# A 1-core transformer kernel: modulation weights summed by VectorE beside the projections, scores of two heads issued together, prefix products ahead of the decays

## The chip, the cores and the metric

The kernel runs on one core of one Trainium2 chip, in one launch. The metric is the device time in microseconds. Three runs of the kernel before have a median of 2638.65 us (2635.41 to 2647.42). The names used below: PE is TensorE, DVE is VectorE, ACT is ScalarE, POOL is GpSimd, SP is SyncE, which here issues all weight loads.

## The reference, cut to what matters

Two blocks are computed on 256 latent tokens and 256 context tokens of width 1024, all in float32. In both, a small vector `c` of 1024 numbers is multiplied with a large matrix `w_mod` (24 MB per layer), and the result shifts, scales and gates the normalised tokens:

```
mod = silu_c @ w_mod[l] + b_mod[l]
sh1, sc1, gt1, sh2, sc2, gt2 = jnp.split(mod[:, None, :], 6, axis=-1)
h = modulate(rms_norm(x, g_pre1[l]), sh1, sc1)
hc = modulate(rms_norm(ctx, g_pre1[l]), sh1c, sc1c)
qn, kn, vn, qh, zf, zb, ih, gh = split_cols(h @ w_in[l])
...
s_win = jnp.einsum('bhrjqd,bhrjakd->bhrjqak', q_blk, k_blk) * scale
p = jax.nn.softmax(s_all, axis=-1)
...
b = jnp.cumsum(log_f.reshape(bsz, nh, n, HG_CHUNK, dk), axis=3)
q_dec = qc * jnp.exp(b)
k_dec = kc * jnp.exp(-b)
def step(s, inp):
    dec, upd = inp
    return dec[..., None] * s + upd, s
```

The first block is: a projection, an attention of 8 heads of 64 over 512 keys, a recurrence in chunks of 32 tokens and both directions ("hgrn"), a projection back, and 16 experts. The second is a hybrid block (the same kind of attention, a delta rule, a gated feed-forward) and a convolution block with another feed-forward.

## The kernel before

Everything is written out by hand: each engine has its own list of instructions, and they meet through semaphores. Each PE result goes to one of eight banks; `next_bank` takes banks in turn from the first `rotating[0]`, and a bank can be filled again once the engine that reads it has counted up `bank_drained`.

All weights pass through `ring`, which has six slots. SP loads them in one fixed order, a slot of 1 MB (some 1.4 or 1.5 MB) at a time; the load with number n first waits until the slot's last user, number n - 6, is done (`freed_by`), and every later load stands behind it in SP's queue. A projection block (`project`, loop over `IN1_BLOCKS`: eight blocks, of which five use four token tiles and three use two) takes two slots; its first slot is freed in the middle of the block, its second at the block's end.

A modulation weight slot ("tile", rows `k`, third `p` of the columns) is used in one of two ways. `modulation_part` has PE multiply it: four matmuls of 32 columns (L476), accumulated over eight tiles in a bank of their own. `weighed_part` gives it to DVE instead (`weigh_modulation`, L1730 for the first tile and L1732 for the others), which adds tile times scalar into a sum kept in the spare ends of the ring's slots; `modulation_sum` then has PE sum over the partitions once, with four matmuls. Before, the 16 tiles "mod1" 1 and 2 (beside blocks n = 0 to 3 of the first projection), the 16 tiles "mod2_0" 0 and 1 (beside the first attention) and the 8 tiles "mod2_1" 0 (beside the second attention) are PE's; "mod2_1" 1 (second attention) and 2 (first feed-forward) are DVE's.

The attention loop (`attention`) runs 16 steps, one for a token tile and a head. In a step PE makes the scores (L785 and L787, or L1364), one modulation tile, the transposes of the probabilities of two steps ago (L455) and the product with the values of three steps ago (L800 or L1377). DVE adds the bias (L1895, first attention only), takes the row maximum (L1898) and copies the transposed probabilities (L1910); ACT takes the exponential (L2828). At steps 7 and 15 DVE also scales a tile's result (L1920), for which it waits for the last values of that tile.

Between the first attention and the recurrence, PE makes the sums of log decays over whole tiles (L834, L839), the chunk decays (L849), the starting states (L860), the prefix and suffix sums in chunks of 32 (L871), transposes (L455) and the chunk products (L889, L909). The recurrence then has eight rounds; a round is eight matmuls for new key-value products (L921, contraction over 32 rows) and eight that read the state (L936, 32 columns), for direction 0 and then direction 1; DVE multiplies and adds into the state (L2070, L2075), twice each a round.

Of the kernel before, what the change touches and what calls it, by code (L numbers as in the profile page):

```python
# [20 lines left out]
P = 128  # L21
# [105 lines left out]
def program(nc, T, out):  # L127
    ctx = ExitStack()
    with ctx:
# [229 lines left out]
        IN1_BLOCKS = (3, 7, 4, 5, 6, 0, 1, 2)  # L359

# [71 lines left out]
        def _(pe):  # L432
# [213 lines left out]
            def attention(tag, n_steps, scores, values, between=None):  # L646

                for i in range(n_steps + 3):
                    if i < n_steps:
                        scores(i)  # L650
                        if between:
                            between(i)
# [10 lines left out]
            def ffn(n):  # L663
                for f in range(FT // 2):
                    for u in range(2):
# [3 lines left out]
                        if u == 0:  # L669
# [3 lines left out]
                            if n == 0 and 1 <= f <= KT:  # L673
                                weighed_part("mod2_1", 2, f - 1)
# [16 lines left out]
                    if n == 0 and f == KT:  # L691
                        modulation_sum("mod2_1", 2, 6, 1)
# [54 lines left out]
            for n, c in enumerate(IN1_BLOCKS):  # L747
# [3 lines left out]
                if n < 4:  # L751
                    for k in range(4 * (n % 2), 4 * (n % 2) + 4):
                        modulation_part("mod1", 1 + n // 2, k, 7 - n // 2, "c1")
                if n == 1:
                    normalised_T("ctx1", CX)
                    transposed("ctx1")
                elif n == 4:
                    modulation_cols("mod1", 1)
                    modulation_cols("mod1", 2)
                elif n == 5:  # L760
                    modulation_gates("mod1")
# [17 lines left out]
            def scores1(i):  # L779
                t, h = divmod(i, NA_HEADS)  # L780
                base = HEAD * (h % 2)
                b = next_bank(("na", i))
                if nth(("na", i)) > 1:
                    pe.wait_ge(bank_drained[bank_of(("na", i))], nth(("na", i)) - 1)
                nc.tensor.matmul(b[:, 0:256], qk(2, h // 2, t * P, P, base), qk(3, h // 2, 0, 256, base), start=True,  # L785
                                  stop=True, skip_group_check=True)
                ins = nc.tensor.matmul(b[:, 256:512], qk(0, h // 2, t * P, P, base), qk(1, h // 2, 0, 256, base),  # L787
                                       start=True, stop=True, skip_group_check=True)
                ins.then_inc(bank_filled[bank_of(("na", i))], 1)
# [34 lines left out]

            for d in range(2):
                if d == 1:
                    heads_T("out1", [MIX[t][0] for t in range(TT)], "nao")
                pe.wait_ge(log_forget_ready, tally.due(log_forget_ready, 4))
                for t in range(TT):
# [8 lines left out]
                    if whole:  # L838
                        ins = nc.tensor.matmul(b, const("ones"), ZC(d, 1 - t), start=False, stop=True,  # L839
                                               skip_group_check=True)  # L840
                        ins.then_inc(bank_filled[bank_of(("hgc", d, t))], 1)
            b = next_bank("decay")
# [22 lines left out]
            for d in range(2):  # L865
                for t in range(TT):
                    for kind in ("pre32", "suf32"):
                        b = next_bank(("hg", kind, d, t))
                        if nth(("hg", kind, d, t)) > 1:
                            pe.wait_ge(bank_drained[bank_of(("hg", kind, d, t))], nth(("hg", kind, d, t)) - 1)  # L870
                        ins = nc.tensor.matmul(b, const(f"{kind}_{d}"), ZL(d, t), start=True, stop=True,  # L871
                                               skip_group_check=True)
                        ins.then_inc(bank_filled[bank_of(("hg", kind, d, t))], 1)
# [38 lines left out]
            for i in range(8):  # L912
                for d in range(2):
                    t, j = divmod(i if d == 0 else 7 - i, 4)
                    rows_ = slice(32 * j, 32 * j + 32)
                    if i < 7:
                        b = next_bank(("hgkv", i, d))
                        if nth(("hgkv", i, d)) > 1:
                            pe.wait_ge(bank_drained[bank_of(("hgkv", i, d))], nth(("hgkv", i, d)) - 1)
                        for h in range(HG_HEADS):  # L920
                            ins = nc.tensor.matmul(b[:, h * P:(h + 1) * P], KLt(d, t)[rows_, h * P:(h + 1) * P],  # L921
                                                   IH(t)[rows_, h * P:(h + 1) * P], start=True, stop=True,
                                                   skip_group_check=True)
                            if h == 3:
                                ins.then_inc(bank_filled[bank_of(("hgkv", i, d))], 1)
                for d in range(2):
                    t, j = divmod(i if d == 0 else 7 - i, 4)
# [3 lines left out]
                    st = R(SBUF_STATE(d, i % 2), HALF)  # L931
                    for h in range(HG_HEADS):
# [425 lines left out]
            def scores2(i):  # L1358
                t, h = divmod(i, 8)
                base = HEAD * (h % 2)  # L1360
                b = next_bank(("gq", i))
                if nth(("gq", i)) > 1:
                    pe.wait_ge(bank_drained[bank_of(("gq", i))], nth(("gq", i)) - 1)
                ins = nc.tensor.matmul(b, R(QBT + (h // 2) * 256 + t * P, P)[base:base + HEAD, :],  # L1364
# [2294 lines left out]
```

## Time and profile before

| what | value |
|---|---|
| median of 3 runs | 2638.65 us |
| the profiled execution's own time | 2635.78 us |
| its span in the trace | 2634.0 us |
| share of the span with PE busy | 81% |
| DVE, ACT, POOL busy | 24%, 13%, 4% |
| mean granted clock of PE | 0.977 of full |
| read from HBM | 751.85 MB, 286 GB/s over the span |

In the order of time: the first projection from 33.6 to 242.6 us, the first attention to 304.6, the work before the recurrence to 349.5, the recurrence to 372.5, the experts (slices with 420 GB/s) from about 420 to 1750, the second attention from 1839.7 to 1899.6, the first feed-forward from 2025.7. A profile's clock of 1.00 is 2.4 GHz, 0.50 is 1.2 GHz. Each fp32 matmul of the program shows as two instructions of PE.

### The profile page before, as it was taken

What the parts mean: (1) busy time and instruction counts of PE and PEld (TensorE: products, weight loads), DVE (VectorE), ACT (ScalarE), POOL (GpSimd) and SP (SyncE); (2) the same over time, 40 slices, a digit from 0 to 9 for tenths busy, and PEclk for the clock granted to TensorE, in tenths of its full rate; (3) what the DMA queues carried; (4) which work ended last, traced back from release to release, by engine and by line L of the source; (5) the groups of instructions that cost most, each with busy time, mean ns of one, the idle gap of its engine ahead of it and who ended that gap; (6) DMA issues with size and microseconds to landing.
All of it is one profiled execution on the core that took longest, in us unless ns stands there. A gap on an engine that the chain in (4) does not pass through costs nothing. (4 is left out here: it accounts for less than half of the span.)

```text
span 2634.0 us, 35391 instructions
## 1 busy us (share of the span) xinstructions
PE 2123.0 (81%) x15628; PEld 1235.5 (47%) x15628; DVE 633.3 (24%) x1157; ACT 343.0 (13%) x692; POOL 96.9 (4%) x116
## 2 busy tenths in 40 slices
PE   7999998555566665667988875579999999999999
PEld 2444664122123222233544432255596884666874
DVE  1122454001011010112312210046653110561000
ACT  2101311000010000011110100022252000131000
POOL 0001000000000000000111100000030000100000
PEclk9999999999999999999999999999899999999999
DMA  9643507999999999999999999963702673314450
GB/s 380 239 166 137 193 33 304 421 424 424 423 424 420 420 424 417 420 406 424 424 424 424 423 424 424 424 253 116 254 3 73 215 267 126 120 65 128 153 201 29
DMA packets 159050, 755.20 MB, mean 287 GB/s; under 512 B 12265, under 2 KB 75881, under 8 KB 102194
## 3 DMA queue, kind: packets, MB, share of 16 engines
q1 hardware_dynamic: 158898, 752.94, 71.8%
q8 instruction: 124, 2.03, 0.3%
q14 instruction: 28, 0.23, 0.0%
HBM read 751.85 MB, written 1.05 MB: 286 GB/s over the span
## 5 line engine op out<-in xcount | busy, mean ns | idle before, releaser
L1208 PE MATMUL psum<-ring,arena 128*32 128x320 f32 x4096 | 358.2, 466 | 282.2 <-DMA ring<-w_up_dram 141.2
L1208 PEld LDWEIGHTS psum<-ring,arena 128*32 128x32 f32 x4096 | 111.4, 110 | 440.7 <-DMA ring<-w_up_dram 173.0
L681 PE MATMUL psum<-arena,ring 128*128 128x256 f32 x1408 | 304.8, 379 | 0.0
L1272 PE MATMUL psum<-ring,arena 128*32 128x512 f32 x1344 | 211.5, 605 | 110.3 <-DMA ring<-w_down_dram 110.3
L681 PEld LDWEIGHTS psum<-arena,ring 128*128 128x128 f32 x1408 | 267.7, 190 | 37.1 <-issue 0.8
L581 PE MATMUL psum<-ring,arena 128*128 128x512 f32 x480 | 215.7, 611 | 7.8 <-ACT arena L2812 3.4
L1272 PEld LDWEIGHTS psum<-ring,arena 128*32 128x32 f32 x1344 | 47.7, 109 | 248.4 <-DMA ring<-w_down_dram 173.7
L2390 DVE TENSOR_TENSOR arena<-arena,psum 128x320 f32<-128x320 f32 (+1 forms) x32 | 16.7, 520 | 583.0 <-PE psum L1208 577.1
L581 PEld LDWEIGHTS psum<-ring,arena 128*128 128x128 f32 x480 | 93.5, 196 | 126.9 <-issue 124.0
L711 PE MATMUL psum<-ring,arena 128*128 128x512 f32 x288 | 125.7, 599 | 0.0
L1217 PE MATMUL psum<-ring,arena 128*32 128x64 f32 x2048 | 119.8, 291 | 0.0
L1217 PEld LDWEIGHTS psum<-ring,arena 128*32 128x32 f32 x2048 | 68.9, 110 | 83.7 <-issue 78.4
L711 PEld LDWEIGHTS psum<-ring,arena 128*128 128x128 f32 x288 | 55.3, 192 | 69.1 <-issue 69.0
L455 PEld LDWEIGHTS psum<-consts,arena 128*128 128x128 f32 x470 | 57.8, 157 | 63.0 <-issue 42.6
L455 PE MATMUL psum<-consts,arena 128*128 128x128 f32 x470 | 74.1, 291 | 15.1 <-DVE arena L2154 3.0
L1943 DVE TENSOR_TENSOR arena<-arena,psum 128x512 f32<-128x512 f32 x22 | 15.1, 687 | 272.7 <-PE psum L681 272.7
L1101 PE MATMUL psum<-arena 128*128 128x128 f32 x544 | 73.0, 283 | 1.3
L476 PE MATMUL psum<-ring,cols 128*32 128x512 f32 x448 | 61.7, 652 | 15.0 <-DMA ring<-w_mod_dram 15.0
L1101 PEld LDWEIGHTS psum<-arena 128*128 128x128 f32 x544 | 64.3, 191 | 16.5 <-issue 16.5
L3087 ACT COPY arena<-psum 128x512 f32<-128x512 f32 x32 | 18.7, 585 | 409.3 <-PE psum L1272 409.3
L3074 ACT ACTIVATE arena<-psum 128x320 f32<-128x320 f32 (+1 forms) x32 | 14.8, 464 | 377.3 <-PE psum L1208 372.8
L1805 DVE TENSOR_TENSOR arena<-psum,gates 128x512 f32<-128x512 f32 x20 | 13.8, 690 | 191.9 <-PE psum L728 131.5
(379 smaller groups left out, 2181.7 us busy)
## 6 DMA issues: line engine op xcount, KB each, us to landing
ring<-w_gate_dram SPq DMA_DIRECT2D x128, 1376.0 KB, 18.1
ring<-w_up_dram SPq DMA_DIRECT2D x128, 1376.0 KB, 18.2
ring<-w_down_dram SPq DMA_DIRECT2D x112, 1536.0 KB, 20.0
ring<-w_mod_dram SPq DMA_DIRECT2D x72, 1024.0 KB, 7.0
ring<-w_ffn_in_dram SPq DMA_DIRECT2D x88, 512.0 KB, 5.2
ring<-w_ffn_out_dram SPq DMA_DIRECT2D x14, 1536.0 KB, 8.7
ring<-w_in_dram SPq DMA_DIRECT2D x16, 1024.0 KB, 7.0
ring<-hyb_w_dram SPq DMA_DIRECT2D x10, 1024.0 KB, 16.7
```

The costliest lines, as they stand in the source:

```text
L455: return nc.tensor.transpose(o, i, const("ident")[0:i.shape[0], 0:i.shape[0]])
L476: ins = nc.tensor.matmul(psum[32 * j:32 * j + 32, bank, :], stat, w[:, j, :], start=(k == 0), stop=(k == KT - 1), skip_group_check=True)
L581: ins = nc.tensor.matmul(banks[t][:, 0:n], XTt(kk, t), w[:, k, :], start=(kk == 0), stop=(kk == 7), skip_group_check=True)
L681: ins = nc.tensor.matmul(b[:, i * 256:(i + 1) * 256], ws[k // 4][:, k % 4, u, i * P:(i + 1) * P], R(XT + k * 256, 256), start=(k == 0), st ...
L711: ins = nc.tensor.matmul(banks[2 * t + c], R(HTF + k * 256 + t * P, P), w[:, (k % 3) * D + c * HALF:(k % 3) * D + (c + 1) * HALF], start=( ...
L1101: ins = nc.tensor.matmul(result(tag)[:, h * P:(h + 1) * P], lhs(h), rhs(h), start=True, stop=True, skip_group_check=True)
L1208: ins = nc.tensor.matmul(banks[u][c][32 * j:32 * j + 32, 0:GMAIN], R(XST + k * HALF + e * CAP, CAP), w3[:, 64 * c:64 * c + 64, QGROUP * j: ...
L1217: ins = nc.tensor.matmul(banks[u][1][32 * j:32 * j + 32, GMAIN:GMAIN + GEXTRA], R(XST + k * HALF + e * CAP, CAP), extra, start=False, stop ...
L1272: ins = nc.tensor.matmul(ybanks[half][32 * c:32 * c + 32, :], stationary, w, start=((half, c) not in begun), stop=(unit >= 36), skip_group ...
L1943: ins = v.tensor_tensor(R(HTF + f * 512, 512), R(SGF + f % 2 * 512, 512), ps, ALU.mult)
L2390: ins = v.tensor_tensor(R(HID + c * GMAIN, n), R(SG + c * GMAIN, n), result(tag)[:, 0:n], ALU.mult)
L3087: a.copy(R(YS + half * HALF, HALF), result(tag)).then_inc(bank_drained[bank_of(tag)], 1)
```

## The change

1. "mod1" 1 and 2 and "mod2_0" 1 go to DVE, spread over all eight blocks of the first projection by `WEIGHED`: two tiles in most blocks and six in blocks n = 2 and n = 3. DVE weighs them between its bank copies, PE makes three sums. The context's transposes move from behind block n = 1 to behind block n = 0, the columns of the modulation from n = 4 to n = 5. SP's order of loads follows.
2. "mod2_1" 1 moves from the second attention to the first feed-forward, where two tiles a pair are now weighed.
3. In both attentions the scores of heads i and i + 1 are issued together every second step, in turn, and five banks rotate instead of four. A modulation tile stands beside every second step only. DVE's scaling of the first tile moves from step 7 to step 9.
4. Before the recurrence, the prefix and suffix sums of a direction follow its log sums at once, over six banks, and come before the chunk decays and states; ACT and DVE follow that order, direction by direction.
5. In the recurrence the matmuls of the two directions are issued in turn, head by head.

```diff
+        WEIGHED = (2, 2, 6, 6, 2, 2, 2, 2)
...
-                if n < 4:
-                    for k in range(4 * (n % 2), 4 * (n % 2) + 4):
-                        modulation_part("mod1", 1 + n // 2, k, 7 - n // 2, "c1")
-                if n == 1:
+                for part in weighed_beside(n):
+                    weighed_part(*part)
+                if n == 0:
                     normalised_T("ctx1", CX)
+                elif n == 1:
                     transposed("ctx1")
+                elif n == 3:
+                    modulation_sum("mod1", 1, 7, 1)
                 elif n == 4:
+                    modulation_sum("mod1", 2, 6, 2)
+                elif n == 5:
...
+                for m in range(2):
+                    nc.tensor.matmul(result(("na", i + m))[:, 0:256], qk(2, h // 2, t * P, P, HEAD * m),
+                                     qk(3, h // 2, 0, 256, HEAD * m), start=True, stop=True, skip_group_check=True)
...
             def between_heads(i):
-                modulation_part("mod2_0", i // KT, i % KT, 4 + i // KT)
-
-            rotating[0] = 4
+                if i % 2 == 0:
+                    modulation_part("mod2_0", 0, i // 2, 5)
+
+            modulation_sum("mod2_0", 1, 4, 0)
+            rotating[0] = 5
...
+                for t in range(TT):
+                    for kind in ("pre32", "suf32"):
+                        b = next_bank(("hg", kind, d, t))
...
+                if d == 0:
+                    heads_T("out1", [MIX[t][0] for t in range(TT)], "nao")
...
+                for h in range(HG_HEADS if i < 7 else 0):
+                    for d in range(2):
...
-                        if j % 8 == 7:
-                            jt = j // 8
+                        for jt in {9: [0], 15: [1]}.get(j, []):
...
-                        weigh_modulation("mod2_1", 2, f, 1)
+                        for p in (1, 2):
+                            weigh_modulation("mod2_1", p, f, p - 1)
...
-                if n < 4:
-                    mod_in("mod1", T["w_mod"], 1 + n // 2, 4 * (n % 2), 4 * (n % 2) + 4)
+                for tag, p, k in weighed_beside(n):
+                    mod_in(tag, T["w_mod"] if tag == "mod1" else T["w_mod_2"][0], p, k, k + 1)
```

SP's queue from the constants' load (behind block n = 1's loads) on, before. `w_in` are a block's two slots, `w_mod` modulation tiles, `g_post` two gains spread over 128 partitions (0.5 MB each); in the brackets stands what the load waits for, and a bank's fill is the end of a block:

```order
L3450 DMA consts<-consts_dram 128x3045
L3460 DMA ring<-w_in_dram 128x4x512 [waits weights_used]
L3460 DMA ring<-w_in_dram 128x4x512 [waits bank2_filled]
L3460 DMA ring<-w_mod_dram 128x2048 [waits weights_used] x3
L3460 DMA ring<-w_mod_dram 128x2048 [waits bank7_filled]
L3450 DMA arena<-g_post_dram 128x1024 x2
L3460 DMA ring<-w_in_dram 128x4x512 [waits weights_used]
L3460 DMA ring<-w_in_dram 128x4x512 [waits bank4_filled]
L3460 DMA ring<-w_mod_dram 128x2048 [waits weights_used] x4
```

The same queue of the change, from the same load to block n = 4's two slots:

```order
L3478 DMA consts<-consts_dram 128x3045
L3488 DMA ring<-w_in_dram 128x4x512 [waits mod_weighed] x2
L3488 DMA ring<-w_mod_dram 128x2048 [waits weights_used]
L3488 DMA ring<-w_mod_dram 128x2048 [waits bank0_filled]
L3488 DMA ring<-w_mod_dram 128x2048 [waits mod_weighed] x2
L3488 DMA ring<-w_mod_dram 128x2048 [waits weights_used]
L3488 DMA ring<-w_mod_dram 128x2048 [waits bank4_filled]
L3478 DMA arena<-g_post_dram 128x1024 x2
L3488 DMA ring<-w_in_dram 128x4x512 [waits mod_weighed] x2
L3488 DMA ring<-w_mod_dram 128x2048 [waits mod_weighed] x4
L3488 DMA ring<-w_mod_dram 128x2048 [waits weights_used]
L3488 DMA ring<-w_mod_dram 128x2048 [waits bank2_filled]
```

Block n = 3's first slot (the second row of `w_in`) stood ahead of every load that waits for the end of block n = 2; now the sixth tile of block n = 2, which waits for that end (`bank4_filled`), and the gains stand ahead of it. The tile that waits for `bank2_filled` stands in the same way ahead of block n = 4's first slot.

PE in the first attention, one step of before (scores, scores, modulation tile, transposes, values):

```order
L785 MATMUL psum<-arena 128x256
L787 MATMUL psum<-arena 128x256
L476 MATMUL psum<-ring,cols 32x512 x4
L455 MATMUL psum<-consts,arena 128x128 x4
L800 MATMUL psum<-arena 128x64 x4
```

and two steps of the change, where L802 and L805 are the scores of two heads:

```order
L802 MATMUL psum<-arena 128x256 x2
L805 MATMUL psum<-arena 128x256 x2
L486 MATMUL psum<-ring,cols 32x512 x4
L465 MATMUL psum<-consts,arena 128x128 x4
L819 MATMUL psum<-arena 128x64 x4
L465 MATMUL psum<-consts,arena 128x128 x4
L819 MATMUL psum<-arena 128x64 x4
```

The first five rows are one step; the seven rows are two steps, so one modulation tile in two has gone, and matmuls of two heads stand side by side.

## Rows read from the trace of the kernel before

**Rows 1.** Timeline of PE, first projection: start us, us, operation, idle before.
```profile
50.21 3.64 PE L476 MATMUL psum<-ring,cols 128*32 128x512 f32 x32
...
76.68 29.38 PE L581 MATMUL psum<-ring,arena 128*128 128x512 f32 x64 [3.42 <-ACT arena L2812]
...
109.55 27.73 PE L581 MATMUL psum<-ring,arena 128*128 128x512 f32 x64
...
185.99 56.80 PE L581 MATMUL psum<-ring,arena 128*128 128x512 f32 x128 [1.79 <-DVE gates L1763]
```

**Rows 2.** DMA issues, 92 to 97.9 us: KB each, median us to landing.
```profile
ring<-w_in_dram SPq DMA_DIRECT2D x1, 1024.0 KB, 5.4
```

**Rows 3.** DMA issues, 123 to 142 us, with pairs issued back to back.
```profile
ring<-w_in_dram SPq DMA_DIRECT2D x6, 1024.0 KB, 7.9
```

**Rows 4.** Windows of PE: stretch, its us, busy (instructions), PEclk, DMA share, GB/s.
```profile
248.70:304.60 55.90, 55.77 (x384) 1.00 0.84 301
1839.70:1899.60 59.90, 54.33 (x297) 0.88 0.80 287
```

**Rows 5.** Timeline of PE, first attention, one step.
```profile
258.87 0.70 PE L785 MATMUL psum<-arena 64*128 64x256 f32 x2
...
259.93 1.07 PE L476 MATMUL psum<-ring,cols 128*32 128x512 f32 x8
260.92 0.66 PE L455 MATMUL psum<-consts,arena 128*128 128x128 f32 x4
261.42 1.00 PE L800 MATMUL psum<-arena 128*128 128x64 f32 x8
```

**Rows 6.** Groups by line, second attention: DVE's weighing; count, busy us, mean ns, idle.
```profile
L1732 DVE SCALAR_TENSOR_TENSOR ring<-ring,cols 128x2048 f32<-128x2048 f32 x7 | 16.5, 2352 | 0.2
```

**Rows 7.** Windows of line L1364 alone (second attention's scores), PE.
```profile
1842.00:1842.02 0.02, 0.02 (x2) 0.50 0.00 0
```

**Rows 8.** Timeline of PE at the start of the second attention.
```profile
1839.67 1.09 PE L1364 MATMUL psum<-arena 64*128 64x512 f32 x2 [1.50 <-ACT arena L3150]
...
1842.00 2.08 PE L1364 MATMUL psum<-arena 64*128 64x512 f32 x4
```

**Rows 9.** Groups by line, first attention: what stands between scores and values.
```profile
L1898 DVE TENSOR_REDUCE small<-psum 128x1 f32<-128x512 f32 x16 | 11.1, 691 | 0.6
L1910 DVE COPY arena<-psum 128x512 f32<-128x512 f32 x16 | 11.1, 691 | 6.2 <-PE psum L455 6.1
L2828 ACT ACTIVATE arena<-psum,small 128x512 f32<-128x512 f32 x16 | 11.0, 687 | 36.3 <-PE psum L455 28.4 <-DVE small L1898 8.0
...
L1895 DVE TENSOR_TENSOR psum<-psum,arena 128x256 f32<-128x256 f32 x16 | 6.9, 432 | 26.8 <-PE psum L787 26.7
```

**Rows 10.** Timeline of PE, between first attention and recurrence.
```profile
314.61 4.09 PE L849 MATMUL psum<-consts,arena 128*128 128x4 f32 x32
318.56 5.44 PE L860 MATMUL psum<-arena 128*128 128x128 f32 x32
323.84 7.03 PE L871 MATMUL psum<-arena,consts 128*128 128x512 f32 x16
...
336.43 3.41 PE L455 MATMUL psum<-consts,arena 128*128 128x128 f32 x16 [2.52 <-ACT arena L2951]
```

**Rows 11.** Timeline of PE, one round of the recurrence.
```profile
352.61 1.71 PE L921 MATMUL psum<-arena 32*128 32x128 f32 x16
354.25 1.53 PE L936 MATMUL psum<-arena 128*32 128x128 f32 x16
```

**Rows 12.** Groups by line, recurrence: one of DVE's two operations on a state.
```profile
L2070 DVE TENSOR_TENSOR arena<-arena,small 128x512 f32<-128x512 f32 x13 | 9.0, 691 | 0.5
```

**Rows 13.** Timeline of SP, first feed-forward: a pair's four half-slot loads, twice.
```profile
2079.46 2.65 SPq L3460 DMA_DIRECT2D ring<-w_ffn_in_dram  x4
...
2093.28 3.33 SPq L3460 DMA_DIRECT2D ring<-w_ffn_in_dram  x4
```

**Rows 14.** DMA issues, 2066 to 2094 us: the modulation tile behind them.
```profile
ring<-w_mod_dram SPq DMA_DIRECT2D x2, 1024.0 KB, 8.5
```

More of the change, by code:

```diff
@@ L359, in program, with weighed_beside, sum_at @@
         IN1_BLOCKS = (3, 7, 4, 5, 6, 0, 1, 2)
+        WEIGHED = (2, 2, 6, 6, 2, 2, 2, 2)
+        def weighed_beside(n):
+            first = sum(WEIGHED[0:n])
+            whole = [("mod1", 1, k) for k in range(KT)] + [("mod1", 2, k) for k in range(KT)]
+            return (whole + [("mod2_0", 1, k) for k in range(KT)])[first:first + WEIGHED[n]]
+        def sum_at(tag, p):
+            return 0 if tag == "mod2_0" else p
         def forget_gates(d):
@@ L912, in _ @@
             for i in range(8):
-                for d in range(2):
[L914 to L925, printed above, removed]
@@ L926, in _ @@
-                for d in range(2):
-                    t, j = divmod(i if d == 0 else 7 - i, 4)
+                for d in range(2 if i < 7 else 0):
+                    next_bank(("hgkv", i, d))
+                    if nth(("hgkv", i, d)) > 1:
+                        pe.wait_ge(bank_drained[bank_of(("hgkv", i, d))], nth(("hgkv", i, d)) - 1)
+                for h in range(HG_HEADS if i < 7 else 0):
+                    for d in range(2):
+                        t, j = divmod(i if d == 0 else 7 - i, 4)
+                        rows_ = slice(32 * j, 32 * j + 32)
+                        ins = nc.tensor.matmul(result(("hgkv", i, d))[:, h * P:(h + 1) * P],
+                                               KLt(d, t)[rows_, h * P:(h + 1) * P],
+                                               IH(t)[rows_, h * P:(h + 1) * P], start=True, stop=True,
+                                               skip_group_check=True)
+                        if h == 3:
+                            ins.then_inc(bank_filled[bank_of(("hgkv", i, d))], 1)
@@ L929, in _ @@
+                for d in range(2):
                     pe.wait_ge(bank_drained[bank_of(("hgkv", i - 1, d) if i else ("hgs", d))],
                                nth(("hgkv", i - 1, d) if i else ("hgs", d)))
-                    st = R(SBUF_STATE(d, i % 2), HALF)
-                    for h in range(HG_HEADS):
+                for h in range(HG_HEADS):
+                    for d in range(2):
+                        t, j = divmod(i if d == 0 else 7 - i, 4)
+                        st = R(SBUF_STATE(d, i % 2), HALF)
@@ L1984, in _ @@
                     v.wait_ge(bank_drained[bank_of(tag)], nth(tag))
-                if n in (1, 3):
-                    modulation_rows("mod1", MB, 1 + n // 2)
-                if n == 1:
+                    if t == 0:
+                        for part in weighed_beside(n)[0:2]:
+                            weigh_modulation(*part, sum_at(*part[0:2]), "c1" if part[0] == "mod1" else "c2")
+                for part in weighed_beside(n)[0 if c in (4, 5, 7) else 2:]:
+                    weigh_modulation(*part, sum_at(*part[0:2]), "c1" if part[0] == "mod1" else "c2")
+                if n == 0:
                     modulated_T("ctx1", 16, 0, 1, XT, 512, 256)
+                elif n == 1:
                     v.wait_ge(bound_ready, tally.due(bound_ready))
@@ L2525, in _ @@
             log_decays(0)
-            def weigh_beside(i):
-                if i % 2:
-                    weigh_modulation("mod2_1", 1, i // 2, 0)
-            attention("gq", False, "gqo", [R(QB + t * HALF, HALF) for t in range(TT)], weigh_beside)
+            attention("gq", False, "gqo", [R(QB + t * HALF, HALF) for t in range(TT)])
             heads_T("out2", QB)
@@ L2908, in _, with key_decays @@
             a.preload_act_table_set("natural_log_exp_and_others")
+            keep_rows("mod2_0", 1)
             attention("na", WP, first_log_forgets)
-            for z_at in forget_gates(1):
-                a.wait_ge(second_input_gate_ready, tally.due(second_input_gate_ready))
-                log_forget(z_at)
             keep_rows("mod2_0", 0)
-            keep_rows("mod2_0", 1)
-            for i in range(4):
+            def key_decays(i):
                 tag = ("hgc", i // 2, i % 2)
@@ L3533, in _ @@
             rows_in(R(BIAS, 4096), T["bias"], bias_loaded)
-            for p in range(2):
-                mod_in("mod2_0", T["w_mod_2"][0], p)
+            mod_in("mod2_0", T["w_mod_2"][0], 0)
             for h in (0, 1):
@@ L3572, in _ @@
             proj_in("hyb", T["hyb_w"], 1536, 512, "z")
-            for k in range(KT):
-                for p in range(2):
-                    mod_in("mod2_1", T["w_mod_2"][1], p, k, k + 1)
+            mod_in("mod2_1", T["w_mod_2"][1], 0)
             for h in (1, 0):
```

115 lines of the change are left out of this document (60 added, 55 removed).

## The prediction

> **What bounds the kernel now.** The table of the page comes first: PE is busy for 81% of the span, DVE for 24%. So I read PE's timeline, stage by stage, for what ends its waits. In the first projection PE runs nearly without a gap; it waits 3.42 us for the context's features and 1.79 for the gates, and a lower clock follows: the block behind the first wait took 29.38 us, the same block at full clock 27.73 [rows 1]. Loads are hidden there; a single slot lands 5.4 us after its issue, and where two are issued back to back the median is 7.9, so I put 2.5 us between them [rows 2, 3]. The experts, which fill the middle, are bound by HBM and untouched. In the first attention PE is busy for 55.8 of 55.9 us, in the second for 54.3 of 59.9, with the clock at 0.88 [rows 4]. A step of the first takes 55.9 / 16 = 3.49 us: scores 1.06, modulation tile 0.99, transposes 0.50 (starts subtracted), values the rest, 0.94 [rows 5]. What PE saves in these stages comes off the end, until something else is late: the experts' loads start behind PE's use of the slots ahead of them, so an earlier PE shifts them too.
>
> **1. First projection.** Removed from PE: 16 tiles, four groups of 3.64 us [rows 1], 14.6. The context's transposes come a block earlier, so their features are ready: 3.4, and 1.65 of clock. Sum -19.6.
>
> Added, by SP's order: block n = 2 now has two slots and six tiles in a ring of six. The sixth tile takes the place of the block's second slot, free only at the block's end, and block n = 3's first slot stands behind it, with the gains (1 MB) between. PE has nothing else to do. It waits for three MB in a row: 5.4 + 2 x 2.5 = 10.4, less 0.3 because SP's issue starts ahead of PE's modelled end: 10.1. From n = 3 to 4 it is two MB, 7.6, with one sum of 1 us hidden in it. After each stall I take 2.4 us of clock, between 1.65 and its double, two low stretches. No other block has this order: with two tiles a block, the load that waits for a block's end is followed by slots needed one block later. Before block n = 6, DVE copies one bank, weighs two tiles of 2.35 us [rows 6], copies the next, and only then the columns and gates: PE starts 5.1 us behind block n = 5, where now it is 2.9: +2.2. The sum of "mod2_0" 1 costs 1.0; that of "mod1" 2 takes the place of the columns. Together 17.7 + 4.8 + 2.2 + 1.0 = 25.7, and with the removed part **+6**. Bounds: stalls of one landing each with one short clock drop, -4; long drops and slow gains, +13. DVE's 24 tiles lie beside blocks of 14 and 28 us.
>
> **2. First attention.** Eight tiles leave: 8 x 0.99 = 7.9. Scores of two heads use rows 0 to 63 and 64 to 127 of PE. Nothing in this stage shows what such neighbours cost, but the second attention has them once: at 1842.00 two matmuls of L1364 run within the same 0.02 us [rows 7], and the two heads' four instructions took 2.08 us at half clock, where one head's two took 1.09 at full clock [rows 8]; so two heads cost as much as one. Saved: 8 x 1.06 = 8.5; with no overlap, zero. Two steps on PE are then 1.06 + 0.99 + 2 x 1.44 = 4.9 us. DVE needs 2 x (0.43 + 0.69 + 0.69), 3.8 with gaps. The chain of a pair: scores are there at 1.35 us, DVE is through with two biases, two maxima and a copy at 4.65, the second exponential (0.69, and 0.19 for its sum) at 5.5 [rows 9]. PE needs it only in the next pair, and the five banks ask for no more, so PE stays the bound. Stage: 8 x 2.05 + 16 x 1.44 + 1.4 for filling and draining = 40.8 against 55.9: **-15**, bounds -7 and -16.
>
> On such neighbours the Trainium skill says (TensorE: Matmul & The Clock Gate, section "Part 3: Packing small matmuls — row/col tiling") that matmuls in different row groups start within 4 ns of each other. By that rule the pair costs what I take from the row; the trace agrees, with both running inside 0.02 us.
>
> **3. Second attention.** The same pairs of scores, 8 x 1.05, and no weighing (8 tiles off DVE), which leaves DVE 2.9 us for 4.9 of PE; nor does DVE wait at step 7 for values just issued. The first exponential comes 6.7 us after the window's start, as before. Then PE has 16 x 1.43, six pairs of scores at 1.05 and six tiles at 1.0: 35.2, and 1.5 for filling: 43.4 against 59.9: **-16.5**, which counts the sum that leaves the window. Bounds: no row overlap, -8; also a shorter low clock behind it, -20.
>
> **4. Before the recurrence.** 44.9 us now, from 304.6 to 349.5, with waits for ACT such as 2.52. In the new order PE has log sums 2.6 and prefix and suffix sums 3.5 (0.87 a matmul, from L871), heads 1.0, the first two again, decays 4.1, states 5.3, transposes 4.1 [rows 10]. Following each bank: direction 1's third prefix bank waits until DVE has copied the heads (13.0 us, where PE would come at 11.6); the starting states end at 24, ACT's eight copies of the transposes at 29.8, where before they ended at 36.3. That is -6.5; a low clock behind that wait gives back 2.5: **-4**, bounds 0 and -8.
>
> **5. Recurrence.** A round takes 1.64 + 1.45 us of PE [rows 11]. In turn, the two directions lie in different rows (L921) or columns (L936), so PE would save about 1.1 a round, 8 in all. But DVE has four operations of 0.69 with gaps of 0.03 a round, 2.9 us against 3.1 [rows 12]. So 0.2 for each of seven rounds: **-1.5**, bounds +1 (PE's gaps bring a low clock) and -3. The Trainium skill has this as a rule against the change (TensorEngine Tiling (Array Packing), section "PSUM Bottleneck"): tiling speeds PE up, not the emptying of PSUM, which may become the bound. By it the recurrence gives 1.5; without it, 8. DVE's row decides for the rule here, and against it in the attentions.
>
> **6. First feed-forward.** One more sum, +1. SP issues a pair's loads every 13.8 us, and 3 MB land within 2.7 + 8.5 = 11.2 us of the first issue [rows 13, 14]. Now a pair has 4 MB; one tile is free earlier, and the other three again need 11.2 of 13.8: hidden, with 2.6 us to spare, and DVE has 5.5 us of work in 13.8. If the cover were gone, it would cost up to 2.5 us in each of eight pairs.
>
> **Sum.** 6 - 15 - 16.5 - 4 - 1.5 + 1 = -30 against the execution's own 2635.8: 2606. The median of the runs shown lies 2.9 above that execution; I say 2608.
>
> **Rivals.** *The row groups don't overlap in these loops*, since waits for banks keep two heads apart: 17 us are lost, 2625. For: the only row is one place, at half clock. Against: both heads' banks are waited for ahead of the pair. 0.10.
> *The ring starves every block, not two*: slower than before. If the next block's slot lands late at five more borders, 5 x (7.6 + 2.4) = 50 us, 2658; it decides with the fifth, where 30 of gain and 13 of margin are gone. For: in five more blocks a tile waits for the end of the block before. Against: SP's order puts the next block's slots ahead of it. 0.05.
> *The two stalls don't come* (the slot is free early): 22 us less, 2586. Against: a queue keeps its order. 0.07.
> *DVE or the chain through ACT bounds the attentions*: 3.0 us a step in place of 2.45, 2 x 16 x 0.55 = 17, 2625. For: scores, maximum, exponential, transpose and copy hang in a row. 0.11.
> *As forecast*: 0.67, with a range of its own from 2596 to 2622.
>
> **Numbers.** The range, 2592 to 2630, takes in both cases at 2625 and leaves out the stalls' absence and the slow case. What a measurement can tell from no change is about 0.5%, 13 us. Faster (under 2625.5) are the forecast, the case without stalls and half of the two at 2625: 0.84; same 0.11; slower 0.05.
>
> **What would show it.** PE's timeline: a wait for `w_in` of about 10 us ahead of the fourth block and 7.6 ahead of the fifth, none elsewhere; halves of a pair of scores that start together; 4.9 us per two steps in both attentions; 2.9 us per round of the recurrence, with DVE never idle; no wait for `w_ffn_in` in the first feed-forward. Wrong would make it: waits at further borders, a step near 3 us, a low clock through the attentions or the recurrence.

## The result

| | before | changed |
|---|---|---|
| median | 2643.03 us (4 runs, 2635.41 to 2647.83) | 2607.08 us (4 runs, 2604.48 to 2612.90) |
| profiled execution, span | 2635.78, 2634.0 | 2612.90, 2611.1 |
| PE, DVE, ACT busy | 81%, 24%, 13% | 80%, 26%, 13% |
| mean granted clock of PE | 0.977 | 0.970 |

The ratio of the changed kernel to the one before is 0.987, with a 95% interval from 0.984 to 0.990. The two profiles aren't equally placed: that of before is nearly the fastest of its four, that of the changed kernel the slowest. So the profiles differ by 22.9 us of span where the medians differ by 36 and the fastest executions by 30.9.

The stages, from the starts of PE's rows in the two traces:

| stage | before, us | changed, us | difference | foretold |
|---|---|---|---|---|
| first attention starts at | 248.67 | 257.99 | +9.3 | +6 |
| first attention | 55.93 | 41.13 | -14.8 | -15 |
| before the recurrence | 44.92 | 39.99 | -4.9 | -4 |
| recurrence | 23.01 | 21.90 | -1.1 | -1.5 |
| recurrence's end to second attention | 1467.14 | 1469.36 | +2.2 | 0 |
| second attention | 59.92 | 44.54 | -15.4 | -16.5 |
| its end to the first feed-forward | 126.15 | 124.53 | -1.6 | 0 |
| the rest, to the span's end | 608.26 | 611.66 | +3.4 | +1 |

Each row compares one execution with one. Stretches with the same PE work differ between profiles. The changed kernel's stretch between the recurrence and the second attention takes 1467.9 to 1470.8 us in its own two profiles and those of the experiments, its last 607.3 to 611.8, and the stage before the recurrence 36.7 to 40.0 where its order is kept.

**The first projection.** PE's timeline of the changed kernel, the part that answers to [rows 1] (start us, us, operation, idle before and who ended it):

```profile
51.06 41.44 PE L591 MATMUL psum<-ring,arena 128*128 128x512 f32 x96 [0.15 <-issue]
103.22 30.22 PE L591 MATMUL psum<-ring,arena 128*128 128x512 f32 x64 [10.72 <-DMA ring<-w_in_dram]
...
141.19 30.01 PE L591 MATMUL psum<-ring,arena 128*128 128x512 f32 x64 [6.75 <-DMA ring<-w_in_dram]
...
172.12 14.00 PE L591 MATMUL psum<-ring,arena 128*128 128x512 f32 x32
...
191.35 57.99 PE L591 MATMUL psum<-ring,arena 128*128 128x512 f32 x128 [1.18 <-DVE gates L1783]
...
255.36 1.94 PE L505 MATMUL psum<-ring,consts 128*32 128x512 f32 x8 [2.53 <-ACT arena L2919]
257.99 1.22 PE L802 MATMUL psum<-arena 64*128 64x256 f32 x4 [0.69 <-ACT rows L2872]
```

Blocks n = 1 and 2 now run as one piece (x96 is 32 + 64 instructions); the wait that the features caused is gone. Two waits for `w_in` stand ahead of the fourth and the fifth block, and nowhere else. The windows of PE around the first of them (stretch, its us, busy, clock, DMA share, GB/s) show what it does to the clock:

```profile
94.60:103.22 8.62, 0.00 (x1) 0.50 0.97 383
103.22:108.20 4.98, 4.98 (x6) 0.50 1.05 417
108.20:133.30 25.10, 25.10 (x59) 1.00 0.39 154
```

The clock is at 1.2 GHz through the last 8.6 us of the wait and the first 5.0 us of the block. Only those 5.0 us cost something, half of them; DMA meanwhile moves 383 to 417 GB/s, so the transfer itself is not slow.

**The attentions.** The windows of PE over both and over the recurrence, as in [rows 4]:

```profile
257.99:299.12 41.13, 40.52 (x320) 0.95 0.61 209
1830.37:1874.91 44.54, 41.88 (x289) 0.92 0.59 197
339.11:361.01 21.90, 16.10 (x241) 1.00 0.00 1
```

PE is still busy for 40.52 of 41.13 us in the first attention. Two of its steps, where [rows 5] has one, and the window of L802 alone over 0.01 us:

```profile
271.24 0.70 PE L802 MATMUL psum<-arena 64*128 64x256 f32 x4
271.77 0.60 PE L805 MATMUL psum<-arena 64*128 64x256 f32 x4
272.30 1.06 PE L486 MATMUL psum<-ring,cols 128*32 128x512 f32 x8
273.30 0.66 PE L465 MATMUL psum<-consts,arena 128*128 128x128 f32 x4
273.79 1.00 PE L819 MATMUL psum<-arena 128*128 128x64 f32 x8
274.63 0.61 PE L465 MATMUL psum<-consts,arena 128*128 128x128 f32 x4
275.08 1.00 PE L819 MATMUL psum<-arena 128*128 128x64 f32 x8
276.01 0.70 PE L802 MATMUL psum<-arena 64*128 64x256 f32 x4
```
```profile
271.24:271.25 0.01, 0.01 (x2) 1.00 0.00 0
```

From 271.24 to 272.30 the scores of two heads take 1.06 us, what one head took before, and two instructions run within the same 0.01 us. The same window at the start of L785 in the kernel before (258.87 to 258.88) has one. The pair repeats every 4.77 us. The second attention repeats every 4.77 as well, but begins worse:

```profile
1837.01 0.66 PE L465 MATMUL psum<-consts,arena 128*128 128x128 f32 x4 [2.47 <-ACT arena L2850]
...
1838.52 1.70 PE L1401 MATMUL psum<-arena 128*128 128x64 f32 x8
1840.15 2.08 PE L1388 MATMUL psum<-arena 64*128 64x512 f32 x4
```

After two pairs of scores PE has nothing left until ACT's first exponential, waits 2.47 us, and the pair behind it takes 2.08 us instead of 1.13: the clock is at 0.51 from 1838.8 to 1845.7.

**Before the recurrence, and the recurrence.** The waits on PE's timeline, as in [rows 10], and two rounds, as in [rows 11]:

```profile
306.66 1.96 PE L854 MATMUL psum<-arena,consts 128*128 128x512 f32 x4 [0.44 <-ACT arena L2963]
...
312.35 1.98 PE L867 MATMUL psum<-arena,consts 128*128 128x512 f32 x4 [1.16 <-DVE arena L2046]
...
330.44 3.81 PE L910 MATMUL psum<-arena 128*128 128x128 f32 x32 [2.22 <-ACT arena L2980]
...
346.54 1.16 PE L942 MATMUL psum<-arena 32*128 32x128 f32 x16
348.44 1.07 PE L958 MATMUL psum<-arena 128*32 128x128 f32 x16 [0.74 <-DVE arena L2101]
349.43 1.16 PE L942 MATMUL psum<-arena 32*128 32x128 f32 x16
```

DVE in the same round (start us, us, operation; an idle time would stand in brackets):

```profile
346.15 0.69 DVE L2101 TENSOR_TENSOR arena<-arena,psum 128x512 f32<-128x512 f32 x1
...
349.05 0.69 DVE L2101 TENSOR_TENSOR arena<-arena,psum 128x512 f32<-128x512 f32 x1
```

The third prefix bank of direction 1 is issued 13.2 us behind the stage's start (299.12), with a wait for DVE's copy of the heads. A round takes 2.89 us, PE's part in it has shrunk from 3.09 to 2.15, and the rest is a wait for DVE, whose four operations follow each other 0.72 us apart without a pause: 2.9 us from the first to the same one of the next round.

**The first feed-forward** has no wait for `w_ffn_in`: up to its sums PE takes 124.48 us, before 124.49. The two sums take 1.93 us, the one of before 1.07.

### The profile page after: what moved, and what is told of

The parts are those of the page before. It is cut to its first block and busy times, and to the rows that moved or that the text cites. A ratio compares the mean times of both kernels' runs of the same rounds, so it can differ in the third digit from the quotient of the medians.

```text
span 2611.1 us, 35133 instructions
## 1 busy us (share of the span) xinstructions
PE 2085.9 (80%) x15460; PEld 1219.8 (47%) x15460; DVE 686.7 (26%) x1181; ACT 343.3 (13%) x692; POOL 97.1 (4%) x116
## 5 line engine op out<-in xcount | busy, mean ns | idle before, releaser
L591 PE MATMUL psum<-ring,arena 128*128 128x512 f32 x480 | 218.5, 617 | 21.4 <-DMA ring<-w_in_dram 17.5
L1752 DVE SCALAR_TENSOR_TENSOR ring<-ring,cols 128x2048 f32<-128x2048 f32 x35 | 82.3, 2352 | 70.7 <-DMA ring<-w_mod_dram 69.9
```

Source lines behind the costliest of these rows:

```text
L591: ins = nc.tensor.matmul(banks[t][:, 0:n], XTt(kk, t), w[:, k, :], start=(kk == 0), stop=(kk == 7), skip_group_check=True)
L1752: ins = v.scalar_tensor_tensor(weighed_sum(i), w, c, weighed_sum(i), ALU.mult, ALU.add)
```

## Experiments

The changed kernel is the base of each. Its own times for comparison are above, and those of its second profile under after_again.

**1. Four tiles beside a block at most.**

```diff
-        WEIGHED = (2, 2, 6, 6, 2, 2, 2, 2)
+        WEIGHED = (2, 2, 4, 4, 4, 2, 4, 2)
...
-                elif n == 4:
-                    modulation_sum("mod1", 2, 6, 2)
                 elif n == 5:
+                    modulation_sum("mod1", 2, 6, 2)
```

> The changed kernel, but with at most four weighed tiles beside a block: WEIGHED is (2, 2, 4, 4, 4, 2, 4, 2). The sum of mod1 2 moves behind block n = 5, because its last tiles are now weighed beside n = 4. Theory (the two stalls come from SP's order: with six tiles, one load that waits for the block's end stands ahead of the next block's first slot): both stalls of the changed kernel's profile, 10.7 and 6.8 us, go, and with them the slower blocks behind them (30.2 and 30.0 us against 27.7 in a block at full clock, 4.8 together); the moved sum and its rows cost some 2 us before n = 6. The first attention starts about 20 us earlier, at 238, and the whole takes 20 us less, 2587. Rival (the stalls come from what has to be read in that time, not from the order of the queue): the same bytes are read in the same 85 us, so waits of some 10 us stay, in other places, and the time is 2597 or more. Second rival (a gain here is lost later): the first attention starts 20 us earlier and the end moves by less than 10.

Measured: a median of 2589.75 us (4 runs, 2580.51 to 2601.16), a ratio of 0.980 to the kernel before (0.976 to 0.985). PE's timeline:

```profile
49.68 68.90 PE L591 MATMUL psum<-ring,arena 128*128 128x512 f32 x160 [0.55 <-issue]
118.51 1.06 PE L505 MATMUL psum<-ring,consts 128*32 128x512 f32 x8
119.51 41.47 PE L591 MATMUL psum<-ring,arena 128*128 128x512 f32 x96
...
167.14 56.87 PE L591 MATMUL psum<-ring,arena 128*128 128x512 f32 x128 [1.79 <-DVE gates L1782]
```

Blocks n = 1 to 5 run with only a sum between them: both stalls are gone, though the same tiles are read. From block n = 1's start to the first scores it takes 231.76 - 49.68 = 182.1 us, where the changed kernel took 257.99 - 51.06 = 206.9. That is 24.8 less, more than the 20 expected. The starts of the rows in both timelines divide it: the two stalls are 17.5, the five blocks 5.2 (nearly all of it the two blocks behind the stalls, which by their own rows are 4.8 slower than 27.73), the moved sum gives 0.2 (I had charged 2 for it; it costs 0.8 before n = 6 and saves the 1.0 behind n = 4), and a clock that stays up in the last two blocks and in the sum of mod2_0 gives 2.0 (57.99 and 1.94 against 56.87 and 1.07). These last 2.0 can't be put down to the missing stalls: experiment 6 has no stalls either, and its last two blocks took 58.05; experiment 4 has both, and its sum took 1.06. The rival (waits in other places, since the bytes are the same) is out: PE waits for no load in this stretch. The medians differ by 17, the second rival asked for under 10. But this kernel's runs fall into two pairs 16 us apart, 2580.5 and 2581.6 with a mean granted clock of 0.978, 2597.9 and 2601.2 with 0.967 and 0.968; the profiled run is the fastest of them, and why two ran at the lower clock isn't known.

**2. Scores of one head per step.**

```diff
-                        if i % 2 == 0:
-                            scores(i)
+                        scores(i)
```

together with the functions `scores1` and `scores2` of before.

> The changed kernel, but the scores of one head are issued in every step, as before, in both attentions; five banks, the halved modulation tiles and DVE's scaling at step 9 stay. Theory (two heads in rows 0 to 63 and 64 to 127 of PE run at the same time, and one head of a pair is free): each attention has 8 x 1.06 = 8.5 us more of PE. The first goes from 41.1 to 49.6 us, the second from 44.5 to 53, and the whole takes 17 us more, 2624. Rival (the gain of the attentions comes from tiles and banks alone, the pair costs what two heads cost): no change in either, 2607. Second rival (PE isn't the bound, the chain through DVE and ACT is): less than 4 us in each attention.

Measured: 2621.82 us (4 runs, 2618.61 to 2624.11), 15 above the changed kernel's median. Two steps of its first attention:

```profile
275.49 0.70 PE L800 MATMUL psum<-arena 64*128 64x256 f32 x2
276.03 0.59 PE L802 MATMUL psum<-arena 64*128 64x256 f32 x2
...
278.97 0.70 PE L800 MATMUL psum<-arena 64*128 64x256 f32 x2
...
281.45 0.70 PE L800 MATMUL psum<-arena 64*128 64x256 f32 x2
```

and PE's first transposes of its second attention, which began at 1838.37:

```profile
1845.12 0.66 PE L465 MATMUL psum<-consts,arena 128*128 128x128 f32 x4 [1.02 <-ACT arena L2844]
```

Two heads cost 2 x 1.06 us, two steps 5.96 against 4.77, and the first attention takes 309.33 - 258.90 = 50.4 us, 9.3 more. The overlap is real and worth what the prediction gave it. The second attention takes only 4.6 more (1838.37 to 1887.50), not 8.5: from the fourth pair on each costs 1.19 more, 5.9 in five, but with single heads the first three pairs take 15.8 us where pairs take 17.1. The pairs leave PE idle for 2.6 us at the start and slow behind it, as shown above; with single heads the wait is 1.02 and the clock 0.78 over the first 7.7 us. This is one profile of the variant, but in every profile with pairs and five banks the second attention takes 44.1 to 44.6 us.

**3. Four banks in both attentions** (`rotating[0] = 4` in place of 5 ahead of each, 5 again behind the second).

> The changed kernel, but four banks rotate instead of five in both attentions; pairs of scores stay. Theory (PE has 4.9 us for two steps, and the chain of a pair in the first attention, from the issue of its scores through bias, maximum and exponential to free banks, takes 5.5, which with four banks falls on PE's path): a pair of the first attention takes 5.5 us or a little more, eight pairs some 5 to 6 us more, 41.1 to about 47; in the second, where no bias is added, the chain is about 4.6 and nothing or 1 us changes. Rival (the fifth bank is of no use): both attentions stay within 0.5 us of 41.1 and 44.5.

Measured: 2610.21 us (one run). Two pairs of the first attention begin at

```profile
275.40 0.70 PE L802 MATMUL psum<-arena 64*128 64x256 f32 x4 [0.86 <-ACT arena L2851]
...
281.10 0.70 PE L802 MATMUL psum<-arena 64*128 64x256 f32 x4 [0.86 <-ACT arena L2851]
```

so a pair takes 5.70 us, and each waits for ACT's exponential to free a bank. The stage takes 45.6 us (255.67 to 301.30), 4.5 more. The fifth bank carries the chain as expected. In the second attention I was off: each pair waits 0.39 us there too (5.23 instead of 4.77), and the stage takes 46.8, 2.3 more; the chain is longer than the 4.6 I had for it. The total of this one run doesn't show the 6.8 us. The first scores came 2.3 us earlier; 0.8 of that is the edit's doing, since the sum of mod2_0 stands in bank 4, which four rotating banks don't use, so that PE needn't wait the 0.69 us for ACT to read it (from the sum's start to the scores 1.86 us, in the changed kernel 2.63). The rest is mostly clock, above all in block n = 0 (13.97 us against 15.36). The stage before the recurrence took 36.7 us (301.30 to 338.03) instead of 40.0, which is clock too.

**4. Directions one after the other in the recurrence** (the loop of before, in place of the one that takes both directions head by head).

> The changed kernel, but the recurrence issues its matmuls for direction 0 and then for direction 1, as before. Theory (DVE's four operations of a round, 2.9 us, bound it in either order, and PE's saving isn't on the path): a round takes 3.1 us instead of 2.89, the stage 1 to 1.5 us more than its 21.9. L921's and L936's counterparts, 1.16 and 1.07 us for both directions in turn, go back to 1.64 and 1.45. Rival (PE's matmuls are the bound of a round in both kernels): the stage goes from 21.9 by 8 x 0.9 = 7 us to 29.

Measured: 2611.80 us (one run).

```profile
348.15 1.71 PE L942 MATMUL psum<-arena 32*128 32x128 f32 x16
349.79 1.53 PE L957 MATMUL psum<-arena 128*32 128x128 f32 x16
351.24 1.71 PE L942 MATMUL psum<-arena 32*128 32x128 f32 x16
```

A round is 3.09 us, without any wait of PE, and the stage 23.0 us, 1.1 more. The sizes were right, but one sentence of the expectation isn't: with the directions apart PE bounds the round, and DVE only with them in turn. DVE's work is the same in both, 9.0 us in 13 of its products, here of this kernel:

```profile
L2095 DVE TENSOR_TENSOR arena<-arena,small 128x512 f32<-128x512 f32 x13 | 9.0, 692 | 0.4
```

So the turn saves PE 0.94 us a round, and 0.2 of it reaches the end. The 1.1 us of the stage are the upper end: where the clock fell in the last round (experiments 1, 2, 3 and 6), its eight state matmuls took 1.66 to 1.92 us instead of 1.07, and the stage 22.5 to 22.8.

**5. The changed kernel again.**

> The changed kernel itself, once more, beside the others of this call, since its first profile was the slowest of four executions (2612.9 against a median of 2607.1). Expected: a median of 2605 to 2609, and in this profile the same stalls of 10.7 and 6.8 us, since they follow from the order of the loads.

Measured: 2609.97 us (5 runs, 2603.81 to 2613.18), ratio 0.988 (0.985 to 0.990), 1 us above the expected range. The stalls in its profile are 10.93 and 6.73 us, as expected from the order of the loads.

**6. The sum under the wait.** Experiment 1, and in it:

```diff
+            modulation_sum("mod2_0", 1, 7, 0)
             for t in range(TT):
                 for kind in ("qT", "kcT", "qrT", "krT"):
                     pe.wait_ge(bank_drained[bank_of((kind, t))], nth((kind, t)))
...
-            modulation_sum("mod2_0", 1, 4, 0)
             rotating[0] = 5
```

> The kernel with at most four weighed tiles beside a block (e1_four_tiles), and the sum of mod2_0 1 moved ahead of PE's last wait before the first attention, into bank 7 instead of bank 4. Theory (that sum, 1.07 us, can lie under the wait of 2.50 us for ACT's copy, and so can ACT's reading of its result, which PE now waits 0.69 us for): the first scores start 1.7 us earlier in relation to the transposes ahead of them; the whole is 1.7 below e1_four_tiles, 2588, and 19 below the changed kernel's median of this call. Rival (DVE is still weighing the last two tiles when the sum is due, which then waits and pushes the rest): no gain over e1_four_tiles, with a wait for DVE ahead of the sum.

Measured: 2583.45 us (5 runs, 2579.96 to 2585.49), ratio 0.978 (0.975 to 0.980). That is 26.5 below the changed kernel measured beside it (experiment 5), where 19 was expected.

```profile
227.38 3.66 PE L465 MATMUL psum<-consts,arena 128*128 128x128 f32 x32
230.96 1.07 PE L505 MATMUL psum<-ring,consts 128*32 128x512 f32 x8
233.54 0.70 PE L802 MATMUL psum<-arena 64*128 64x256 f32 x4 [1.51 <-ACT arena L2918]
```

The transposes' start to the first scores is 6.16 us, in experiment 1 it was 7.92 (223.84 to 231.76): 1.76 saved, as foretold, and no wait for DVE. The total fell by 6 against experiment 1's median. Experiment 1's four runs spread over 20 us and weren't taken beside these, so I claim 1.8 of it. The gain over the changed kernel measured beside it, 26.5, lies where it should: from block n = 1's start to the first scores it is 181.5 us (52.04 to 233.54) against 206.95 (51.28 to 258.23), 25.4 less. Over that stretch it is only 0.6 below experiment 1, because the last two blocks took 58.05 us here and 56.87 there.

**7. The gains loaded later.**

```diff
-                elif n == 2:
+                elif n == 4:
                     post_rows(T["g_post1"], T["g_post2"])
```

> The changed kernel, but the two gains (1 MB) are loaded behind block n = 4's tiles instead of between block n = 2's last tile and block n = 3's first slot. Theory (PE's stall ahead of n = 3 is the landing of three MB in a row, 5.4 + 2 x 2.5): it is 2.5 us shorter, 10.7 to 8.2; the stall ahead of n = 4, which has two MB and not the gains in it, stays at 6.8. Rival (the two halves land side by side and the queue's bandwidth is not what PE waits for, only the latency of one load): 10.7 stays.

Measured: 2602.86 us (one run).

```profile
100.91 29.84 PE L591 MATMUL psum<-ring,arena 128*128 128x512 f32 x64 [8.09 <-DMA ring<-w_in_dram]
...
138.41 29.87 PE L591 MATMUL psum<-ring,arena 128*128 128x512 f32 x64 [6.66 <-DMA ring<-w_in_dram]
```

The first stall falls from 10.93 (experiment 5, measured beside it) to 8.09, by 2.84 for 1 MB, and the second stays. PE waits for what stands ahead in the queue. With 2 MB the stall is now 8.09; the second one, also 2 MB, is 7.7 with the sum that lies in it (130.69 to 138.41).

**8. The old order before the recurrence**, on PE, DVE and ACT; on PE:

```diff
             for d in range(2):
+                if d == 1:
+                    heads_T("out1", [MIX[t][0] for t in range(TT)], "nao")
...
-                for t in range(TT):
-                    for kind in ("pre32", "suf32"):
...
+            (the same loop behind the starting states)
```

> The changed kernel, but between the first attention and the recurrence all three engines keep the order of before: log sums, heads, chunk decays, starting states, and only then the prefix and suffix sums. Theory (the new order lets ACT and DVE work on direction 0 while PE is busy with the rest): the stage, from the first log sum to the first matmul of the recurrence, goes from 40.0 us back to 44 to 45, with the wait of 2.5 ahead of the transposes back. Rival (the stage's gain came from six rotating banks, which this kernel keeps): 40 to 41.

Measured: 2610.26 us (one run). The stage takes 341.17 - 297.49 = 43.7 us, 3.7 more than in the changed kernel, and its waits are

```profile
302.39 1.06 PE L465 MATMUL psum<-consts,arena 128*128 128x128 f32 x8 [2.11 <-ACT rows L2873]
...
322.67 1.09 PE L465 MATMUL psum<-consts,arena 128*128 128x128 f32 x8 [0.88 <-DVE arena L2077]
325.61 1.94 PE L465 MATMUL psum<-consts,arena 128*128 128x128 f32 x8 [1.84 <-ACT arena L2975]
330.04 6.28 PE L911 MATMUL psum<-arena 128*128 128x128 f32 x32 [2.49 <-ACT arena L2975]
```

The order makes the gain, not the banks: the rival foretold 40 to 41 and is out. The stage came 0.3 us below the expected range. The clock blurs the size: of the changed kernel's 40.0 us some 3.3 are low clock, which shows beside experiment 3, the same order with the clock up:

```profile
316.35 3.63 PE L879 MATMUL psum<-consts,arena 128*128 128x4 f32 x32
319.84 3.82 PE L890 MATMUL psum<-arena 128*128 128x128 f32 x32
```

The changed kernel's own rows for these two lines have 4.70 and 6.00. Here L911, with 6.28 instead of 3.81, has 2.5 of it. Without the clock the orders would be 36.7 and 41.2 (an estimate from these rows, one profile each), 4.5 apart.

## Why the prediction was right, and where its terms were off

The forecast was 2608 us, the median 2607.1, and the mechanisms are those foretold. That the two numbers lie within 1 us is luck. The forecast's -30 has three measured values beside it: -22.9 (the profiles, of which that of the changed kernel is its slowest execution), -30.9 (the fastest executions, 2635.4 and 2604.5) and -36 (the medians). And it was added to a median of before that a fourth run then moved from 2638.65 to 2643.03. Three of the terms (both attentions and the stage before the recurrence) came close because errors in what PE has to do and in the clock cancelled, as told below.

**First projection, +6 foretold, +9.3 measured.** Both stalls came at the two borders that SP's order names, 10.7 and 6.75 us against 10.1 and 6.6 net of the sum. Experiment 1 removes them by changing only how many tiles stand between, experiment 7 shortens one by 2.84 us for 1 MB, where I had 2.5. The clock behind them cost 2.5 and 2.3 (30.22 and 30.01 against 27.73), against 2.4 each. Block n = 6 starts 5.4 us behind block n = 5 (191.35 - 185.96), foretold 5.1. What the term missed is mostly late: the sum of mod2_0 was priced at 1.0 us at full clock, but it stands behind a wait of 2.53 and took 1.94 at half clock; ACT then has to read its bank before the attention begins (0.69); and the last two blocks took 57.99 against 56.80. With 0.9, 0.7 and 1.2 us these are 2.8; 0.8 more is in the stalls and 0.3 ahead of n = 6. Against these 3.9 stands the first block, 15.36 us where before it took 16.70 for the same matmuls. That is clock, and chance: the same block takes between 13.97 and 16.72 us in the other profiles. The 1.2 of the last two blocks isn't the stalls' doing, since they take 57.7 to 58.1 us in every profile of the changed kernel and its variants but experiment 1's, with and without stalls; what causes it stays open. The sum's clock and its reader's time are one oversight: PE waits for the sum's reader, and a short sum behind a wait may run at half clock (it did in six profiles with 1.93 or 1.94 us, of this kernel and its variants; in experiments 1 and 4 it took 1.07 and 1.06 behind the same wait of 2.50). Experiment 6 moves the sum under that wait and gets 1.8 back.

**First attention, -15 and -14.8.** Experiment 2 shows the two parts: the row overlap is worth 9.3 (8.5 foretold), and the rest, 5.5, is the eight tiles (7.9) less the low clock at the start of that profile. A pair takes 4.77 us, foretold 4.9, because the transposes that stand directly behind values take 0.45. That the stage came out at the foretold size is chance in part: with the clock up it takes 39.3 us (experiments 1, 4 and 6), 1.5 below the forecast of 40.8, and a low clock at its start, which no term had, put 1.8 back. With four banks it would be 5.70, where I had put the chain at 5.5 (experiment 3); so what keeps the rival away in which the chain bounds the attention is the fifth bank, worth 0.9 us a pair. (The 4.65 us in the working of that chain don't follow from its rows, which give 1.35 + 2.93 = 4.28 without gaps.) The Trainium skill (TensorE: Matmul & The Clock Gate, section "Part 3: Packing small matmuls — row/col tiling") has matmuls of different row groups start within 4 ns; in the 0.01 us window above two of them run, so the trace agrees as far as a window of 10 ns can tell.

**Second attention, -16.5 and -15.4.** PE's first transposes came 6.64 us behind the first scores (1837.01 - 1830.37, foretold 6.7), so the wait was in the forecast. The clock behind it was not: 0.51 for 6.9 us costs 3.4. Pairs that are 0.13 faster give back 1.0 of it, and what is left of the difference to 44.5 us, 1.3, is filling that I had added (1.5) and that was hardly needed. The 1.6 us won behind this attention are clock as well: before, it was at 0.50 for 17 us from 1895.9 on, now for 10 us from 1876.4.

**Before the recurrence, -4 and -4.9; recurrence, -1.5 and -1.1.** The wait at the third prefix bank came at 13.2 us (foretold 13.0) with 1.16; experiment 8 gives 3.7 back of the 4.9, or 4.5 where the clock is taken out. The -4 was -6.5 for the order and 2.5 for a low clock; measured are 36.7 us with the clock up (experiments 3 and 7), which is -8.2, and 3.3 for the clock. The rule of the Trainium skill that I weighed here (TensorEngine Tiling (Array Packing), section "PSUM Bottleneck") held: PE's part of a round fell by 0.94 us, and DVE's four operations on the results, 2.89 us, set the round. Experiment 4 puts the worth of the turn at 1.1 us at most, not 8.

**First feed-forward, +1.** No wait for weights came: the cover was there, as foretold, and the second sum costs 0.9. But from the feed-forward to the end the profiles differ by 3.4 us. 1.2 of it lies in the convolution block (30.57 us against 29.40 for the same matmuls), and the remaining 1.3 can't be told from chance: with the same code there, experiment 8's profile takes 607.3 us to the end, less than the 608.3 of before, and experiment 2's 611.8. The same holds for the 2.2 between the recurrence and the second attention, a stretch that the change leaves alone and that takes 1467.9 to 1470.8 us in the nine profiles of the changed kernel and its variants.

## What to carry to other kernels

In a ring that one queue fills in order, count what stands between a block's last slot and the next block's first: one load that waits for a block's end holds back everything behind it, and the 1 MB that was moved out of the way there had cost 2.8 us of PE. Spreading the same loads so that every block's slots and tiles fit the ring together turned 17.5 us of stalls into nothing.

Price a saving on one engine by the engine that is next: pairs of scores gave all of their 9 us because PE stayed the bound and a fifth bank took the chain off its path, while the same kind of overlap in the recurrence gave at most 1 of 8.

A short piece of work behind a wait is better moved under it: a sum of 1.07 us took 1.94 behind a wait of 2.5 in most profiles, and its reader 0.69 more.

Compare stages over several profiles before giving a difference of 1 to 3 us a cause: here the same matmuls took up to 3.3 us more in one profile's stage than in another's, with the clock.

## What the hardware did that was not expected

The low clock belongs as much to the stall as to what follows. With a stall of 10.7 us, the granted clock was 0.50 for 13.6 us, of which 8.6 lay in the stall itself; the block lost 2.5 us. Behind the stall of 6.75 us the block lost 2.3. The longer stall hardly cost more clock, and the other profiles agree: behind stalls of 10.64 to 10.93 us the block took 29.25 to 30.27 us, behind 8.09 it took 29.84, behind 6.66 to 6.99 it took 29.49 to 30.01.

Issuing more in parallel can start a stage worse. With pairs of scores PE reached the first dependent transposes early, waited 2.6 us and lost 3.4 to the clock; with single heads it waited 1.0 us, and the same first six heads took 1.4 us less (experiment 2).
